# Nine expert-weight tiles instead of seven, rows picked straight from the residual stream, in a two-layer hybrid encoder

## The reference: what is computed

```python
h = rms_norm(x, norm2_g[l])                       # x * rstd(row) * gain(column)
g_sel = argmax(h @ w_rg + b_rg)                   # one of 4 groups
top_val, top_idx = top_k(e_logits[tok, g_sel], 2) # 2 of its 8 experts
gate = p_group * softmax(top_val)
# for each of 32 experts e, over the tokens routed to it:
y = (silu(xb @ w_gate[e]) * (xb @ w_up[e])) @ w_down[e]   # 1024 -> 512 -> 1024
x = x + sum of gate * y over a token's two experts
```

## Time and profile before

| what | value |
|---|---|
| median of 3 runs | 1734.57 us (1732.05 to 1737.44) |
| the profiled execution's own time | 1733.59 us |
| its span, first to last instruction | 1731.7 us |
| TensorE matmuls, share of the span | 1614.3 us, 93% |
| DVE, ScalarE, GpSimd busy | 37%, 24%, 18% |
| HBM read and written | 447.54 MB and 18.88 MB, 269 GB/s over the span |
| mean granted TensorE clock | 0.98 of full |
| chain that ended last | TensorE 70%, DMA 16%, DVE 10% |

### The profile page before, as it was taken

The page is one execution under the profiler, slowest core; times in us unless marked ns, Lnnn a source line. Parts: engine busy times, 40 slices in busy tenths (PEclk is TensorE's granted clock), DMA queues, the critical chain, the costliest instruction groups (busy, mean ns, idle before and its releaser), DMA issues.

```text
span 1731.7 us, 20238 instructions
## 1 busy us (share of the span) xinstructions
PE 1614.3 (93%) x8312; PEld 850.6 (49%) x8312; DVE 636.6 (37%) x1098; ACT 411.5 (24%) x690; POOL 305.5 (18%) x374
## 2 busy tenths in 40 slices
PE   8989979989999999997798999798899999999985
PEld 4645656456444444443356556555554444444422
DVE  1784565451111111111329756665411111112115
ACT  3464731211111111110134547302011111111101
POOL 5920680000000000000269008600000000000003
PEclk9999999989999999999999999999899999999998
DMA  7000402559999999999840003035699999999996
GB/s 311 1 1 1 147 1 37 206 237 388 403 421 430 428 428 427 428 428 428 335 183 1 1 22 126 1 101 227 242 365 427 419 428 427 429 428 427 428 428 259
DMA packets 57008, 469.87 MB, mean 271 GB/s; under 512 B 17841, under 2 KB 17969, under 8 KB 30386
## 3 DMA queue, kind: packets, MB, share of 16 engines
q1 hardware_dynamic: 44866, 444.35, 62.1%
q10 hardware_dynamic: 9744, 15.80, 2.4%
q0 software_dynamic: 2304, 8.39, 1.4%
HBM read 447.54 MB, written 18.88 MB: 269 GB/s over the span
## 4 chain that ended last, share of the span: by engine, by line
PE 70%; DMA 16%; DVE 10%; ACT 2%; issue 1%; POOL 1%; ACTq 0%; POOLq 0%; DVEq 0%
PE bank L884 20%; DMA ring<-wu 14%; PE bank L552 10%; PE bank L877 8%; PE bank L920 8%; PE bank L688 5%; PE bank L861 2%; PE bank L627 2%; PE bank L642 2%; PE bank L614 2%; DMA expert_rows<-raw_qd 1%; PE bank L523 1%; DVE ring L1378 1%; PE bank L906 1%; PE bank L730 1%
## 5 line engine op out<-in xcount | busy, mean ns | idle before, releaser
L885 PE MATMUL bank<-ring,hbuf 128*64 128x512 f32 x1024 | 456.1, 599 | 0.0
L884 PE MATMUL bank<-ring,hbuf 128*64 128x512 f32 x704 | 312.8, 598 | 19.4 <-DMA ring<-wu 17.9
L1787 DVE COPY raw_qd<-bank 128x256 f32<-128x256 f32 x64 | 27.2, 425 | 758.0 <-PE bank L906 758.0
L920 PE MATMUL bank<-ring,raw_qd 128*64 128x512 f32 x512 | 233.4, 598 | 6.2 <-DVE raw_qd L1787 6.2
L922 PE MATMUL bank<-ring,raw_qd 128*64 128x512 f32 x512 | 233.4, 598 | 0.0
L2030 POOL DMA_INDIRECT raw_qd<-expert_rows,dest_i x12 | 11.7, 975 | 1180.4 <-DMA expert_rows<-raw_qd 1177.3
L552 PE MATMUL bank<-hbuf,ring 128*128 128x512 f32 x480 | 210.8, 596 | 0.0
L877 PE MATMUL bank<-raw_qd,hbuf 128*128 128x256 f32 x896 | 207.3, 385 | 0.0
L884 PEld LDWEIGHTS bank<-ring,hbuf 128*64 128x64 f32 x704 | 95.6, 138 | 216.9 <-issue 216.9
L877 PEld LDWEIGHTS bank<-raw_qd,hbuf 128*128 128x128 f32 x896 | 165.9, 190 | 24.0
L884 PE MATMUL bank<-raw_qd,hbuf 128*64 128x512 f32 x320 | 142.5, 599 | 10.9 <-DMA ring<-wu 9.5
(11 more groups left out here) (346 smaller groups left out, 2003.2 us busy)
## 6 DMA issues: line engine op xcount, KB each, us to landing
ring<-wu SPq DMA_DIRECT2D x64, 2048.0 KB, 17.9
ring<-wd SPq DMA_DIRECT2D x64, 2048.0 KB, 16.7
ring<-wg SPq DMA_DIRECT2D x44, 2048.0 KB, 20.3
raw_qd<-wg SPq DMA_DIRECT2D x20, 2048.0 KB, 18.8
ring<-w_in SPq DMA_DIRECT2D x8, 2048.0 KB, 16.0
expert_rows<-raw_qd ACTq DMA_DIRECT2D x120, 128.0 KB, 8.7
ring<-w_out SPq DMA_DIRECT2D x4, 2048.0 KB, 13.5
x<-x_in SPq DMA_DIRECT2D x4, 512.0 KB, 5.3
```

The source lines that it names most:

```text
L884: mm(pb[2 + par][0:CAP, :], tokens[:, k, :], gates[k], start=(k == 0), stop=(k == KT - 1))
L885: last = mm(pb[2 + par][CAP:P, :], tokens[:, k, :], W_up[par][:, k, :], start=(k == 0), stop=(k == KT - 1))
L920: mm(pb[5 + par][0:CAP, :], hidT[par][:, k, :], W_down[par][:, k, 0:512], start=(k == 0), stop=(k == FT - 1))
```

## The change

It does these things:

- **Tiles.** Nine weight tiles: slots 0 to 5 are the ring, 6 to 8 are the former spare tile, the first half of `hbuf` (where `h` was) and a new buffer `ninth`, whose first quarter is the former `gB`. Expert e uses slots 3(e mod 3) to 3(e mod 3)+2.
- **Order of loads on SP.** d2 after `rho` (in place of the gain row), u2 after `o_c`, g2 after `dest`; then for e from 3 on g, u, d of the same expert.
- **No `h`.** `h_row` is gone. TensorE picks from `x`. The selection matrix carries `rstd` in place of 1 and is built in twelve instructions per group in place of eight. The gain is applied by ScalarE as a per-partition scale when a part leaves PSUM, for which a part takes four activations (first group) or two (others) in place of one.
- **`kept`.** After expert 29's rows ScalarE writes `x * rstd` for the overflow path (not taken for this input: no instruction of it is in the trace). The DVE waits for these four activations ahead of the gathered rows.
- **Places.** Hidden rows of odd experts lie on partitions 64 to 127; GpSimd's temporaries move to `ninth`, and its waits on `r_done` and `ho` go.
- **Scratch.** `dynamic_dma_scratch_size=4096` when the program is built.

```diff
+        ninth = sb("ninth_slot", [P, 4096])
+        gB = ninth[:, 0:D]
...
+        corner = [ident[CAP * i:CAP * i + CAP, CAP * i:CAP * i + CAP] for i in range(2)]
...
-        h = hbuf[:, 0:4096].rearrange("p (b d) -> p b d", b=NB)
+        kept = hbuf[:, 0:4096].rearrange("p (b d) -> p b d", b=NB)
...
             sp.wait_ge(s["rho"], on("rho") + 1)
-            sp.dma_start(gB[:, :], gains[layer]).then_inc(s_gain, 16)
+            base = layer * NE
+            sp.dma_start(slot_tile[8], wd[base + 2]).then_inc(slot[8], 16)
             sp.wait_ge(s["y5"], on("y5") + 1)
...
+            sp.wait_ge(s["o_c"], on("o_c") + 2)
+            sp.dma_start(slot_tile[7], wu[base + 2]).then_inc(slot[7], 16)
             sp.wait_ge(s["wo"], on("wo") + 4 * NB)
...
-            for e in range(2, NE):
-                at = 3 * (e % 2)
-                if e < 3 or e > LEADING:
-                    gates(e)
-                sp.wait_ge(s["gu"], e - 1)
-                sp.dma_start(ring[:, at + 1, :], wu[layer * NE + e]).then_inc(slot[at + 1], 16)
-                if 2 <= e < LEADING:
-                    gates(e + 1)
-                if e >= 3:
-                    down(e - 1)
-            down(NE - 1)
-
-            sp.wait_ge(s["h2"], on("h2") + NB)
+            sp.dma_start(slot_tile[6], wg[base + 2]).then_inc(slot[6], 16)
+            for e in range(3, NE):
+                at = 3 * (e % 3)
+                sp.wait_ge(s["gu"], e - 2)
+                sp.dma_start(slot_tile[at], wg[base + e]).then_inc(slot[at], 16)
+                sp.dma_start(slot_tile[at + 1], wu[base + e]).then_inc(slot[at + 1], 16)
+                sp.wait_ge(s["dn"], e - 2)
+                sp.dma_start(slot_tile[at + 2], wd[base + e]).then_inc(slot[at + 2], 16)
...
-                        last = mm(pb[n % 2][:, P * i:P * i + P], h[:, b, P * k:P * k + P], pick[0][:, b, slots],
+                        last = mm(pb[n % 2][:, P * i:P * i + P], x[:, b, P * k:P * k + P], pick[0][:, b, slots],
...
-            pe.wait_ge(s["h2"], on("h2") + NB)
...
-                    A(xT[0][:, 4 * at:4 * at + 4, P * half:P * half + P],
-                      pb[n % 2][:, :].rearrange("p (k c) -> p k c", k=4), ACT.Copy).then_inc(s["xp_e"], 1)
+                    for i in range(4):
+                        k = 4 * at + i
+                        ins = A(xT[0][:, k, P * half:P * half + P], pb[n % 2][:, P * i:P * i + P], ACT.Copy,
+                                scale=gain2[:, k:k + 1])
+                    ins.then_inc(s["xp_e"], 1)
                     return
-                A(flat(xT[group % 2][:, 2 * part:2 * part + 2, :]), pb[n % 2][:, :], ACT.Copy).then_inc(s["xp_e"], 1)
+                for i in range(2):
+                    k = 2 * part + i
+                    ins = A(xT[group % 2][:, k, :], pb[n % 2][:, GC * i:GC * i + GC], ACT.Copy, scale=gain2[:, k:k + 1])
+                ins.then_inc(s["xp_e"], 1)
...
+                if e == KEPT_AT:
+                    act.wait_ge(s["gu"], KEPT_AT + 1)
+                    for b in range(NB):
+                        A(kept[:, b, :], x[:, b, :], ACT.Copy, scale=rstd[:, b:b + 1]).then_inc(s["kept"], 1)
...
-            h_row(0)
-            h_row(1)
...
-            h_row(2)
...
-            h_row(3)
...
                 for b in range(NB):
-                    ins = TS(pick[group % 2][:, b, :], slot_ids, of[:, b:b + 1], None, ALU.is_equal)
+                    TS(pick[group % 2][:, b, :], slot_ids, of[:, b:b + 1], rstd[:, b:b + 1], ALU.is_equal, ALU.mult)
+                    ins = TS(second[:, b, :], slot_ids, of[:, NB + b:NB + b + 1], rstd[:, b:b + 1], ALU.is_equal, ALU.mult)
                 link(ins)
                 for b in range(NB):
-                    STT(out=pick[group % 2][:, b, :], in0=slot_ids, scalar=of[:, NB + b:NB + b + 1],
-                        in1=pick[group % 2][:, b, :], op0=ALU.is_equal, op1=ALU.add).then_inc(s["oh"], 1)
+                    TT(pick[group % 2][:, b, :], pick[group % 2][:, b, :], second[:, b, :], ALU.add).then_inc(s["oh"], 1)
...
+            dve.wait_ge(s["kept"], on("kept") + NB)
             gathered_rows(0)
...
             pool.wait_ge(s["s5p"], on("s5p") + 32)
-            pool.wait_ge(s["r_done"], on("r_done") + 5)
-            pool.wait_ge(s["ho"], on("ho") + 2)
...
-    nc = bacc.Bacc("TRN2", target_bir_lowering=False, num_devices=1)
+    nc = bacc.Bacc("TRN2", target_bir_lowering=False, num_devices=1, dynamic_dma_scratch_size=4096)
```

More of the change, by code:

```diff
@@ L50 @@
 LATE = NE - 2
+KEPT_AT = NE - 3
 NROWS = LATE * CAP + 1
@@ L203, in trunk @@
         slot_ids = raw[:, 6656:6656 + GC]
+        squares = [raw[:, at:at + D] for at in (2048, 4096, 5120, 7168)]
+        second = raw[:, 2048:3072].rearrange("p (b s) -> p b s", b=NB)
         pick_o, pick_ot = (raw[:, 7168 + 256 * i:7424 + 256 * i].rearrange("p (b s) -> p b s", b=NB) for i in range(2))
@@ L216, in trunk @@
         weighted, weighted_t = (raw[:, 2048 + 512 * i:2560 + 512 * i].rearrange("p (b s) -> p b s", b=NB) for i in range(2))
-        selT = [gB[:, 512 * i:512 * i + 512] for i in range(2)]
+        selT = [tile(raw, at) for at in (3584, 4608)]
         rel_late = small[:, 8:16]
@@ L277, in trunk @@
             wo="PE: output projection groups", res="DVE: residual added", rms2="ACT: norm 2 root mean squares",
-            h2="DVE: h rows", h2t="PE: x^T of a block",
+            kept="ACT: rows of x times inverse root mean squares kept for overflow blocks", h2t="PE: x^T of a block",
             h2_d="DVE: x^T of a block, first half evacuated", h2_a="ACT: second half evacuated",
@@ L352, in trunk, with loaded @@
         w_o = [ring[:, 4 + i, :].rearrange("p (k c) -> p k c", k=KT) for i in range(2)]
[L353 to L359, removed]
+        THIRD = (raw_qd[:, 7168:11264], hbuf[:, 0:4096], ninth[:, :])
+        slot_tile = [ring[:, i, :] for i in range(6)] + list(THIRD)
+        W_gate = [slot_tile[3 * i].rearrange("p (k c) -> p k c", k=KT) for i in range(3)]
+        W_up = [slot_tile[3 * i + 1].rearrange("p (k c) -> p k c", k=KT) for i in range(3)]
+        W_down = [slot_tile[3 * i + 2].rearrange("p (k c) -> p k c", k=FT) for i in range(3)]
+        def loaded(slot_, e, layer):
+            before = (1 if slot_ in (4, 5) else 0) if 3 <= slot_ < 6 else len(range(slot_ // 3, NE, 3)) * layer
+            return 16 * (before + e // 3 + 1)
         NU = QH // 2 * NB
@@ L525, in tensor_program @@
                         last.then_inc(s["pe"], 1)
-            loaded = layer * 16 + 16
+            win_loaded = layer * 16 + 16
             def group(n):
@@ L532, in group @@
                 if c == 0:
-                    pe.wait_ge(s_win[i], loaded)
+                    pe.wait_ge(s_win[i], win_loaded)
                 if n >= KT + 4:
@@ L890, in gate_up @@
                 at = CAP * (e % GRP)
[L891 to L897 removed]
+                i = 3 * (e % 3)
+                pe.wait_ge(slot[i], loaded(i, e, layer))
                 pe.wait_ge(s["xp_e"], 2 if e < 2 else GRP * (e // GRP) + GRP)
@@ L929, in down @@
                     pe.wait_ge(s["ye"], e - 1)
-                down_of(e % 2, 16 * (LOADS[3 * (e % 2) + 2] + e // 2 + 1 + (0 if e % 2 else NE // 2 * layer)))
+                pe.wait_ge(slot[i], loaded(i, e, layer))
+                down_of(e % 2, W_down[e % 3])
             def weights_turned(i):
@@ L2050, in _ @@
                     sp.wait_ge(s_fd, b + 1)
-                    sp.dma_start(out[P * b:P * b + P, :], h[:, b, :]).then_inc(s_out, 16)
+                    sp.dma_start(out[P * b:P * b + P, :], kept[:, b, :]).then_inc(s_out, 16)
                 sp.wait_ge(s_out, 16 * NB)
```

112 lines of the change are left out of this document (44 added, 68 removed).

## The result

The changed kernel took 1741.67 us, median of 9 runs (1738.34 to 1743.91); the kernel before took 1733.16 beside it (9 runs, 1730.87 to 1737.44). The ratio is 1.0043, 95% interval 1.0032 to 1.0053: **slower by 8.5 us**, above the 0.3% that the prediction called measurable. The forecast was 1738.6, 5.0 us more than before. The sign and the range hold, and so do the early shift, the hole in the loads and the order at the end as causes. But 3.5 us of size are missing, because the layer ends on another path than the one that the sum followed. The profiled execution after has a span of 1741.9 us against 1731.7 before, mean granted clock 0.975 against 0.980.

The account below looks back on a forecast made before the run. The DMA was taken as the slower side, 15.35 us per expert against TensorE's 14.49. Shift +2.6 less tiles 1.5 ends weights 1.1 us later; with the order, +2.5 us per layer: 1733.6 + 5.0 = 1738.6 us, range 1723 to 1750.

Parts of the forecast that it names:

- the early shift: TensorE's early steps in a layer: selection and evacuation prices less h_row's gain, +2.6 us, bounds +0.9 and +3.7.
- the hole in the loads: SP's list: d4 waits for `dn` 2 until 415.25 with g5, u5 behind it; no weight DMA between about 407 and 417.
- the order at the end: End of layer: d29 ahead of u30, +5.1 us for that tile; store of 29's rows lands +2.5 us, shift and tiles included.
- h_row, 0.1 us: Routing: removing four instructions of 4.96 us per layer gains only 0.1 us, since TensorE is what is late next.
- Selection, +1.06 per layer: First group's matrix ahead of the first pick: eight TENSOR_SCALAR instead of four at 0.264 us, +1.06 us; bound +2.1.
- Evacuation, +0.84 twice: ScalarE, first group: four scaled copies of 0.36 us instead of one of 0.60, +0.84 us before experts 0 and 2.
- clock term: TensorE's early steps: longer idle may add low-clock time, less work at the low level takes away; within 1 us.
- The tiles, -1.5 per layer: Weight loads: 20 tiles are there at 450.9 instead of 452.4 us, so nine tiles win 1.5 us before the shift.
- rival B: Weight loads: the two extra tiles stay ahead, 10.2 us more weights loaded at 450 us, about -6 us per layer, 1722; chance 0.12.
- the sign of being right: End of layer: the last store landing in 5.5 to 8 us would show the forecast right.
- A: End of layer: store gains nothing from the emptier queue, everything moves with u30, 6.2 us per layer, 1746; chance 0.16.
- The rest: `kept` activations hidden, or 4 us once per layer; GpSimd's dropped waits held nothing; hidden rows on other partitions: same shapes.

Follow-up runs that it names:

- e5: Changed kernel with four dead instructions of h_row's form put back at h_row's places; 1741.58 us, 1.0039 of the kernel before.
- e4: Kernel before, seven tiles and their order kept, with h_row gone and the changed selection, picks from x, scaled evacuations and kept rows; 1738.82 us, ratio 1.0028.
- e3: Changed kernel with gate and up tiles of expert e+1 issued ahead of e's down tile only from e = 20; 1734.73 us, 1.0002 of the kernel before.
- e1: Changed kernel with gate and up tiles of expert e+1 issued ahead of e's down tile, from expert 3 on; 1717.19 us, 0.9898 of the kernel before.
- e8: Kernel before with only the smaller scratch for GpSimd's DMAs (4096); 1733.41 us, ratio 0.9994.
- e9: Changed kernel with gate and up tiles of e+1 ahead of e's down tile only up to e = 28; 1720.13 us, 0.9915 of the kernel before.

## Why the prediction was right, and where 3.5 us were missing

**h_row, 0.1 us: right.** Idle for TensorE in the changed kernel's timeline, and e5.

**Selection, +1.06 per layer: too small.** Eight at 0.323 us apart, where 0.264 was taken and 0.397 was the bound; the picks start at 362.19, 1.4 us later after the 0.45 is taken off. The step that chose the lower end "since the columns and the source are those of L1726" looked at the shape and not at the form. The Trainium skill (VectorE: DVE Perf Modes, "The perf-mode tier table") gives tensor_scalar on float32 in SBUF one pace, with no exception for two scalars, so by it the pace of L1726 would have stayed; the trace does not agree, 0.323 against 0.264.

**Evacuation, +0.84 twice: too large.** +0.55 twice: four scaled activations of 128 columns end 1.14 us after the first begins and not 1.44, since they overlap. With the selection that makes 1.4 + 1.1 = 2.5 us of shift against the forecast's 2.6: two errors that cancel, which is luck. And 2.5 is not what arrives: gate and up of expert 2 start at 399.43 against 397.04, 2.4 later or 1.9 after the 0.45. The window of the changed kernel that answers to rows 9 is

```profile
360.00:370.00 10.00, 7.81 (x57) 7.81 (x58) 9.21 (x35) 1.14 (x4) 0.00 (x0) 0.74 0.00 0
```

About 5.2 us of it are at the lower level (10 x 0.26 x 2), but TensorE idles in the first 2.2 of them, so 3.0 us of picks ran there; before it were 4.6 less 0.3, 4.3. That gives back 1.3 / 2 = 0.6 us, an estimate that closes the sum: the "less work at the low level" of the forecast's clock term. e4 gives 5.7 us for two layers by the medians and 4.9 by the ratios; 2 x 1.9 lies inside its interval.

**The tiles, -1.5 per layer: right within the noise.** e3 has the nine tiles, the hole and the old order at the end; e4 has the seven tiles; both have the shift. By the ratios they differ by 0.26%, 4.5 us, 2.3 per layer (4.1 and 2.0 by the medians), for a forecast of 1.5. And the reason given, that SP's wait for `dn` 2 takes the head start back, is what e1 shows: without it the nine tiles win (1.0028 - 0.9898) x 1733 = 22.5 us, 11 per layer. That is the 10.2 us of rival B. B was the right value of two free tiles, and what spoke against it, the wait, is why it didn't come.

**The order at the end, +1.4 per layer net: the term that was mis-sized.** Two things in it. The store of 29's rows came near its forecast in sum: GpSimd starts the gathers at 846.22 against 844.71, +1.5 for a forecast of +2.5. But two misses cancel in that. The landings of its two halves, issued at 836.4 and 836.9, are

```profile
DMA to landing us min/median/max: 6.9/7.7/8.4
```

8.4 us for the later one, where 7.0 was taken, 5.5 to 8 was to be the sign of being right and 8.5 the threshold of A. And it was issued only 3.9 us later than before (836.43 against 832.58), where 6.2 was forecast, since gate and up of 30 had waited less and ran at the higher clock (first the changed kernel, then the one before):

```profile
824.11 0.61 PE L872 MATMUL bank<-ring,hbuf 128*64 128x512 f32 x1 [1.94 <-DMA ring<-wu]
```

```profile
818.61 1.09 PE L884 MATMUL bank<-ring,hbuf 128*64 128x512 f32 x1 [3.63 <-DMA ring<-wu]
```

So A as it stood, everything moving by 6.2 us with u30, did not happen; but a part of its size came on the other path. The step that failed is "the combining matmuls move from 858.0 to 864.2, still before the last adds that began at 864.97". The DVE's list has the first combined add long before the last ones, at 857.42, behind four of eight gathered adds; it needs the first block's matmuls, which end 2 us after the start, not the last block's. The slack was 4.4 us, and the combining moved by 7.2. And it was counted for layer 1 only: "the second layer repeats the pattern" is not so there, where the slack was 0.4 us. By the distances from the gathers this step is worth the 1.3 and 2.4 us of the section on the result, 3.7 in all, the size of what is missing. Carry: layer 1 hands on 3.3 us (L541 at 877.85 against 874.57), selection in layer 2 makes 5.2 of it at the picks (1222.4 against 1217.2), gate and up of 31 start 9.4 later, and the combining's wait turns that into 10.1. By e3 the order's price is 6.9 us for both layers against the forecast's 2 x 1.4.

**The clock, ±1 us in the shift: right there, and missing at the end.** In the shift it gave back about 0.6 us, as above. Windows of the changed kernel while gate and up of 31 run, both layers, and of the kernel before at the same work:

```profile
839.00:843.00 4.00, 3.59 (x10) 1.42 (x12) 0.00 (x0) 2.85 (x3) 0.00 (x0) 0.58 0.92 381
1700.00:1707.00 7.00, 6.28 (x16) 2.06 (x18) 0.00 (x0) 3.18 (x4) 0.00 (x0) 0.53 0.58 239
```

```profile
833.00:837.00 4.00, 3.10 (x16) 1.33 (x18) 0.00 (x0) 0.00 (x0) 0.00 (x0) 1.00 0.99 422
1692.00:1697.00 5.00, 5.00 (x19) 1.79 (x16) 0.00 (x0) 0.00 (x0) 0.00 (x0) 0.66 1.01 426
```

In layer 1 TensorE had waited 3.65 us before this work and was granted the lower level (1.2 GHz) for about the first 3.5 us of it; before, it had waited 2.00 us and kept the higher one. The stretch at the lower level is not new in that layer: before, it stood one expert earlier, behind the wait of 3.63 us at 818.61, where the next wait for a tile could take it up and the store of 29's rows could not. After, it is the other way round. In layer 2 both had waited 3.6 us (3.63 and 3.64), and the lower level lasted longer after the change. From the start of gate and up to the combining that is 1.7 us in layer 1 (5.5 later becomes 7.2) and 1.2 in layer 2 (9.4 becomes 10.6). What sets the length of the low stretch no run here separates: e3's trace has the same 0.53 from 1693 to 1700 us, behind the same wait of 3.64.

**The rest: right.** The scratch costs nothing (e8), and the gathers' pace is as before. The kept rows are written from 837.58 to 841.84, while ScalarE has nothing to do before 848.23. The hidden rows' partitions and GpSimd's dropped waits had no run of their own; e4 has neither, so whatever they cost or win is inside the difference that is called the tiles.

So the likeliest case was the right one in its terms, and its number fell on the other side of 0.3% by a slack read off at the wrong add: +5 forecast, +8.5 measured. By the medians e4 gives 5.7 to the shift, e3 against e4 takes 4.1 back, and the changed kernel against e3 adds 6.9; by the ratios it is 4.9, 4.5 and 7.1, together 7.5. The forecast for both layers was 5.2, 3.0 and 2.8. Each measured step is uncertain by 2 to 3 us.

## What to carry to other kernels

More buffers are worth little while the queue that fills them is a list in which a load whose slot is free stands behind one whose slot isn't. Write the issues in the order in which the slots come free, which here is also the order in which the tiles are needed; the same nine tiles were worth 2 us per layer in one order and 11 in the other. And where two paths meet, read the slack at the first instruction that needs both, in each layer by itself.

## What the runs showed of the hardware beyond what was expected

- TENSOR_SCALAR on 128x256 float32 with a scalar from SBUF: 0.264 us apart with one operation and one scalar, 0.323 with two operations and two scalars. Of the two-tensor forms at the same size, SCALAR_TENSOR_TENSOR with one scalar runs 0.397 us apart, TENSOR_TENSOR without one about 0.34 (four in 1.43 us). So 0.06 us goes with a further scalar in either form; what of it is the scalar and what the further operation no run separates.
- Four scaled activations of 128x128 out of PSUM end 1.14 us after the first begins; one of 512 columns takes 0.60. One cost TensorE's stall 0.73 us, four 1.28.
- The same stall of 3.6 us was followed by a stretch at the lower clock that differed in length: in layer 2, 0.66 in the mean over 5 us before, 0.53 over 7 us after. A stall of 2.0 us (before, 833.90) or 1.94 us (after, 824.11) was followed by none.
- The store of 29's rows landed 8.4 us after its issue in the changed kernel and 10.76 before, 10.56 in e1 and 6.8 in e9: it has no one price.
